# Moving the four tiles of split inputs to byte 352 of their 512-byte period

## The chip, the cores and the metric

One NeuronCore of a Trainium2 chip runs the whole program. The metric is the device time of one execution in microseconds. Lower is better.

## What is computed

One sequence of 256 tokens with 1024 features goes through two transformer blocks in float32. The first has two attentions (stick-breaking and latent), an output projection, a gated feed-forward part with a short convolution, and a gated embedding. The second has a sparse attention, a convolution branch and a memory attention, which are gated and merged, and a gated feed-forward part. Cut to what matters here:

```
h = rms_norm(x) ; proj = h @ w_in ; ... attention ... ; x = x + rms_norm(mix @ w_o)
h = rms_norm(x) ; u = causal_depthwise_conv(h @ w_up)
x = x + rms_norm((gelu(gate) * val) @ w_down)
x = x + rms_norm(sigmoid(rms_norm(x) @ w_ple_gate + b) * (p @ w_ple))
... second block: xn @ w_in, three branches, merged @ w_out ...
x = h + (silu(hn @ w_gate) * (hn @ w_up)) @ w_down
```

Nearly all of the arithmetic is in these products of an activation with a weight matrix.

## The kernel before

Every weight matrix is cut into 128x128 blocks. Eight blocks make one weight tile of 1024 columns, which is loaded into `raw`. ScalarE rounds it to the fp32r type in `whi` (L1109), and VectorE (L1622) or GpSimd (L602) writes what the rounding lost to `wlo`. The activations are split in the same way: ScalarE writes the rounded half (L1132) and VectorE what is left (L1651, L1881, L2245). Both halves of one 128-feature chunk lie side by side in a row of 512 floats, columns 0 to 255 high and 256 to 511 low.

A block product is then three matmuls, of which the weights are the stationary operand and the activation the moving one (256 columns, 1024 bytes per partition):

```
nc.tensor.matmul(dst, wh, hi, ...)   # L619
nc.tensor.matmul(dst, wl, hi, ...)   # L620
nc.tensor.matmul(dst, wh, lo, ...)   # L621
```

The helper `blk3` issues them. TensorE runs its instructions in the order of the program text, and each matmul has a weight load of its own (128 columns, 512 bytes per partition), which the profile lists as PEld. A few stages with the tokens in the rows (`tm`, L662 to L664) have the roles turned round: there the activation is the stationary operand and up to 512 weight columns move.

Four tiles hold split activations:

- `HA`, the normed input of most stages (eight chunks);
- `HB`, a second one of that size (attention outputs, the merged branches);
- `HL`, half as long (latent inputs, the convolution branch, the sparse attention's output);
- `ACTS`, the 22 chunks of feed-forward activations, which shares its place with the attention's tiles (`QS`, `QM`, `Z`, `CW` and others), since those are dead by then.

SBUF tensors are laid one behind the other in the order of the text, each start rounded up to 32 bytes. Tensors that nothing reads (`before_ha`, `before_hb`, `before_hl`, `behind_hl`) stand between them as spacers. Of the addresses this text gives the *phase*: the byte address within the partition, modulo 512. `whi` and `wlo` have phase 128, and since a block is 512 bytes wide, so has every weight block. A chunk of a split tile is 2048 bytes and a half 1024, so all hi and lo operands of one tile have that tile's phase.

| tile | address before | phase before | address after | phase after |
|---|---|---|---|---|
| raw, whi, wlo | 16512, 36992, 61568 | 128 | the same | 128 |
| X, Y, SQ | 87936, 96128, 104320 | 384 | the same | 384 |
| HA | 112960 | 320 | 112992 | 352 |
| HB | 129472 | 448 | 129888 | 352 |
| HL | 146048 | 128 | 146784 | 352 |
| KMEM to identb | 154496 and on | 384 | 155040 and on | 416 |
| ACTS, YC, G1, PX and most attention tiles | 173376 and on | 320 | 173920 and on | 352 |
| QME, U, CY, PR2, OMEM, TH | 200992 and on | 288 | 201536 and on | 320 |

Before, the split tiles and ACTS start at multiples of 64 bytes. Phase 352 is 32 bytes past such a multiple.

Of the kernel before, what the change touches and what calls it, by code (L numbers as in the profile page):

```python
# [16 lines left out]
P = 128  # L17
# [281 lines left out]
def program(nc, stream, xT, memT, pT, pos, consts, w2, out):  # L299
    ctx = ExitStack()  # L300
    with ctx:
        def sb(name, shape, dt=F32):
            return ctx.enter_context(nc.sbuf_tensor(name, shape, dt))
# [9 lines left out]
        X = sb("X", [P, DC, S])  # L313
        Y = sb("Y", [P, DC, S])
        SQ = sb("SQ", [P, DC, S])
        sb("before_ha", [P, 112])
        HA = sb("HA", [P, DC, 2 * S], F32R)
        sb("before_hb", [P, 32])
        HB = sb("HB", [P, DC, 2 * S], F32R)
        sb("before_hl", [P, 48])  # L320
        HL = sb("HL", [P, 4, 2 * S], F32R)
        sb("behind_hl", [P, 64])
        KMEM = sb("KMEM", [P, MEMH, S])
        VMEM = sb("VMEM", [P, QT, 512])
        RTT = sb("RTT", [P, 2, 2 * S])
# [2102 lines left out]
```

## Time and profile before

| what | value |
|---|---|
| median of three executions | 882.14 us (881.25 to 884.82) |
| the profiled execution, its time | 886.73 us |
| its span, first to last instruction | 885.0 us |
| mean granted TensorE clock | 0.988 |
| TensorE matmul busy | 832.1 us, 94% |
| TensorE weight load busy | 794.3 us, 90% |
| VectorE busy | 660.9 us, 75% |
| ScalarE busy | 499.7 us, 56% |
| GpSimd busy | 321.6 us, 36% |

A matmul is on record for longer than it keeps the next one waiting, since matmuls are pipelined. What one costs is read from the distance between two starts, or from the number of them in a stretch in which TensorE never sits idle. A granted clock of 1.00 is the 2.4 GHz level, 0.50 the 1.2 GHz level.

### The profile page before, as it was taken

How to read it: one execution, taken by the hardware profiler on the slowest of the kernel's cores; microseconds unless marked ns; L12 is line 12 of the kernel's file. 1: busy time of each engine (PE TensorE's matmuls, PEld its weight loads, DVE VectorE, ACT ScalarE, POOL GpSimd, SP SyncE). 2: the span in 40 equal slices, each digit the busy share in tenths (PEclk: the TensorE clock that was granted, in tenths of full speed). 3: DMA queues.
4: the chain of work that ended last, by engine and by line, in shares of the span. 5: the costliest groups of instructions: out<-in, count | busy, mean ns of one | idle time of the engine just before them, and what ended most of it. 6: DMA issues, size and time to landing. Idle time of an engine off the chain costs nothing.

```text
span 885.0 us, 16964 instructions
## 1 busy us (share of the span) xinstructions
PE 832.1 (94%) x6722; PEld 794.3 (90%) x6722; DVE 660.9 (75%) x981; ACT 499.7 (56%) x914; POOL 321.6 (36%) x148
## 2 busy tenths in 40 slices
PE   4999999999899999998999889988999999999998
PEld 3998889899899999797999779877998899999998
DVE  6695863898889997657899988865756576667774
ACT  6665645844555666866765574457555545444441
POOL 3743222112332333443656453422454233323321
PEclk8999999999999999999999998999999999999999
DMA  5743234344564756461756452322445457666651
GB/s 206 267 161 98 76 91 141 117 144 158 168 213 149 222 160 190 142 190 49 247 168 201 152 171 73 96 96 72 137 153 168 163 152 224 196 190 192 185 173 49
DMA packets 57246, 137.18 MB, mean 155 GB/s; under 512 B 6352, under 2 KB 27088, under 8 KB 57168
## 3 DMA queue, kind: packets, MB, share of 16 engines
q1 hardware_dynamic: 57168, 136.11, 48.4%
q8 instruction: 53, 0.87, 0.4%
q14 instruction: 25, 0.20, 0.1%
HBM read 135.03 MB, written 1.05 MB: 154 GB/s over the span
## 4 chain that ended last, share of the span: by engine, by line
PE 57%; DVE 23%; ACT 9%; issue 7%; DMA 2%; POOL 1%; SPq 0%; DVEq 0%; ACTq 0%
PE PROD L619 11%; PE PROD L620 10%; PE PROD L621 10%; DVE wlo L1622 6%; DVE YC L1930 5%; ACT whi L1109 4%; DVE RS L1630 3%; PE PROD L681 3%; PE OP L821 2%; DMA raw<-stream 2%; PE OP L619 2%; PE TP L621 2%; PE TP L620 2%; PE TP L619 2%; PE OP L621 2%
## 5 line engine op out<-in xcount | busy, mean ns | idle before, releaser
L602 POOL TENSOR_TENSOR wlo<-raw,whi 128x1024 fp32r<-128x1024 f32 x124 | 318.2, 2572 | 542.8 <-ACT whi L1109 518.6
L619 PE MATMUL PROD<-HA,whi 128*128 128x256 f32 x1080 | 306.8, 284 | 14.4 <-DVE HA L1651 6.0
L620 PE MATMUL PROD<-HA,wlo 128*128 128x256 f32 x1080 | 301.8, 279 | 0.0
L621 PE MATMUL PROD<-HA,whi 128*128 128x256 f32 x1080 | 301.7, 279 | 0.0
L1109 ACT ACTIVATE whi<-raw 128x1024 fp32r<-128x1024 f32 x252 | 261.8, 1053 | 39.7 <-PE PROD L621 21.1
L1622 DVE TENSOR_TENSOR wlo<-raw,whi 128x1024 fp32r<-128x1024 f32 x128 | 192.7, 1510 | 77.8 <-ACT whi L1109 77.7
L619 PEld LDWEIGHTS PROD<-HA,whi 128*128 128x128 f32 x1080 | 205.8, 191 | 17.7 <-DVE HA L1651 6.4
L620 PEld LDWEIGHTS PROD<-HA,wlo 128*128 128x128 f32 x1080 | 205.5, 190 | 0.6 <-issue 0.5
L621 PEld LDWEIGHTS PROD<-HA,whi 128*128 128x128 f32 x1080 | 205.1, 190 | 0.0
L1930 DVE SCALAR_TENSOR_TENSOR YC<-Y,CV,YC 128x255 f32<-128x255 f32 x88 | 66.9, 762 | 2.2 <-ACT YC L1333 0.7
L619 PE MATMUL OP<-HA,whi 128*128 128x256 f32 x200 | 57.2, 286 | 1.5 <-DVE wlo L1622 0.8
L621 PE MATMUL OP<-HA,whi 128*128 128x256 f32 x200 | 56.1, 281 | 0.0
L620 PE MATMUL OP<-HA,wlo 128*128 128x256 f32 x200 | 56.1, 280 | 0.0
L1630 DVE RECIPROCAL RS<-RTT 128x256 f32<-128x256 f32 (+2 forms) x18 | 42.9, 2382 | 15.8 <-ACT RTT L1128 15.7
L619 PE MATMUL SC<-ACTS,whi 128*128 128x256 f32 x176 | 49.1, 279 | 4.1 <-POOL wlo L602 2.4
L681 PE MATMUL PROD<-SQ,ones 128*128 128x256 f32 x144 | 37.3, 400 | 13.2 <-ACT SQ L1121 13.2
L621 PE MATMUL SC<-ACTS,whi 128*128 128x256 f32 x176 | 48.8, 277 | 0.0
L620 PE MATMUL SC<-ACTS,wlo 128*128 128x256 f32 x176 | 48.8, 277 | 0.0
L619 PE MATMUL TP<-ACTS,whi 128*128 128x256 f32 x176 | 48.7, 277 | 0.0
L620 PE MATMUL TP<-ACTS,wlo 128*128 128x256 f32 x176 | 48.7, 277 | 0.0
L621 PE MATMUL TP<-ACTS,whi 128*128 128x256 f32 x176 | 48.7, 277 | 0.0
L681 PEld LDWEIGHTS PROD<-SQ,ones 128*128 128x128 f32 x144 | 26.6, 197 | 21.2 <-issue 10.0
(322 smaller groups left out, 1648.4 us busy)
## 6 DMA issues: line engine op xcount, KB each, us to landing
raw<-stream SPq DMA_DIRECT2D x197, 512.0 KB, 4.0
raw<-stream SPq DMA_DIRECT2D x144, 128.0 KB, 2.4
raw<-stream SPq DMA_DIRECT2D x28, 256.0 KB, 2.9
raw<-stream SPq DMA_DIRECT2D x4, 384.0 KB, 3.4
X<-xT SPq DMA_DIRECT2D x2, 512.0 KB, 5.6
out<-X SPq DMA_DIRECT2D x8, 128.0 KB, 2.0
KMEM<-memT SPq DMA_DIRECT2D x1, 512.0 KB, 5.4
VMEM<-memT SPq DMA_DIRECT2D x1, 512.0 KB, 6.1
```

What stands on the lines that cost most here:

```text
L602: nc.gpsimd.tensor_tensor(wlo[:, n % NSPLIT, :], raw[:, n % NRAW, :], whi[:, n % NSPLIT, :].bitcast(F32), ALU.subtract).then_inc(lo_pool, 1)
L619: nc.tensor.matmul(dst, wh, hi, start=start, stop=False, skip_group_check=True)
L620: nc.tensor.matmul(dst, wl, hi, start=False, stop=False, skip_group_check=True)
L621: last = nc.tensor.matmul(dst, wh, lo, start=False, stop=stop, skip_group_check=True)
L681: last = nc.tensor.matmul(dst[:, 0:w], mat[:, :], chunks[i][:, 0:w], start=i == 0, stop=i == len(chunks) - 1)
L821: last = nc.tensor.matmul(OP[:, j * dv:(j + 1) * dv], PT[0:w, i * P:(i + 1) * P], v, start=kb == 0, stop=kb == nkb - 1, skip_group_check=True)
L1109: nc.scalar.activation(whi[:, n % NSPLIT, :], raw[:, n % NRAW, :], ACT.Copy).then_inc(hi_done, 1)
L1622: nc.vector.tensor_tensor(wlo[:, n % NSPLIT, :], raw[:, n % NRAW, :], whi[:, n % NSPLIT, :].bitcast(F32), ALU.subtract).then_inc(lo_vector, 1)
L1630: nc.vector.reciprocal(dst[:, 0:width], RTT[:, RT[name] % 2, 0:width]).then_inc(rs_ready, 1)
L1930: ins = nc.vector.scalar_tensor_tensor(out=y[:, shift:S], in0=src[:, 0:S - shift], scalar=CV[:, at:at + 1], in1=y[:, shift:S], op0=ALU.mul ...
```

## The change

Only the widths of the four spacers change, so that HA, HB, HL and ACTS all start at phase 352. No instruction is added, removed or moved on any engine, and every tensor behind HA moves up by 32 to 736 bytes.

```diff
         SQ = sb("SQ", [P, DC, S])
-        sb("before_ha", [P, 112])
+        sb("before_ha", [P, 120])
         HA = sb("HA", [P, DC, 2 * S], F32R)
-        sb("before_hb", [P, 32])
+        sb("before_hb", [P, 124])
         HB = sb("HB", [P, DC, 2 * S], F32R)
-        sb("before_hl", [P, 48])
+        sb("before_hl", [P, 124])
         HL = sb("HL", [P, 4, 2 * S], F32R)
-        sb("behind_hl", [P, 64])
+        sb("behind_hl", [P, 16])
         KMEM = sb("KMEM", [P, MEMH, S])
```

## Rows read from the trace of the kernel before

**Rows 1.** The page: busy time by engine, and the chain that ended last.
```profile
span 885.0 us, 16964 instructions
PE 832.1 (94%) x6722; PEld 794.3 (90%) x6722; DVE 660.9 (75%) x981; ACT 499.7 (56%) x914; POOL 321.6 (36%) x148
...
PE 57%; DVE 23%; ACT 9%; issue 7%; DMA 2%; POOL 1%; SPq 0%; DVEq 0%; ACTq 0%
```

**Rows 2.** Groups by line and shape, L619's five: busy, mean ns, idle before.
```profile
L619 PE MATMUL PROD<-HA,whi 128*128 128x256 f32 x1080 | 306.8, 284 | 14.4 <-DVE HA L1651 6.0 <-DVE HA L1881 2.2 <-ACT CW L1477 1.8
...
L619 PE MATMUL OP<-HA,whi 128*128 128x256 f32 x200 | 57.2, 286 | 1.5 <-DVE wlo L1622 0.8 <-DVE KS L1707 0.5 <-DVE HA L1651 0.3
...
L619 PE MATMUL SC<-ACTS,whi 128*128 128x256 f32 x176 | 49.1, 279 | 4.1 <-POOL wlo L602 2.4 <-DVE ACTS L1651 1.5
...
L619 PE MATMUL TP<-ACTS,whi 128*128 128x256 f32 x176 | 48.7, 277 | 0.0
...
L619 PE MATMUL PROD<-HB,whi 128*128 128x256 f32 x160 | 45.4, 284 | 0.0
...
L619 PE MATMUL PROD<-HL,whi 128*128 128x256 f32 x68 | 20.1, 296 | 2.2 <-DVE HB L2245 2.2
```

**Rows 3.** Timeline of TensorE: HB (phase 448), nine steps in 1.02 us.
```profile
679.94 0.28 PE L621 MATMUL PROD<-HB,whi 128*128 128x256 f32 x1
...
680.96 0.28 PE L621 MATMUL PROD<-HB,whi 128*128 128x256 f32 x1
```

**Rows 4.** Timeline of TensorE: HL (phase 128), nine steps in 1.08 us.
```profile
361.84 0.28 PE L621 MATMUL PROD<-HL,whi 128*128 128x256 f32 x1
...
362.92 0.28 PE L621 MATMUL PROD<-HL,whi 128*128 128x256 f32 x1
```

**Rows 5.** Timeline of TensorE: HA (phase 320), nine steps in 1.06 us.
```profile
320.69 0.28 PE L619 MATMUL PROD<-HA,whi 128*128 128x256 f32 x1
...
321.75 0.28 PE L619 MATMUL PROD<-HA,whi 128*128 128x256 f32 x1
```

**Rows 6.** Windows without idle time: busy (count) of PE, PEld, DVE, ACT, POOL, clock.
```profile
44.00:54.80 10.80, 10.80 (x94) 10.80 (x93) 9.40 (x10) 6.92 (x12) 3.45 (x2) 1.00 0.26 90
241.00:257.40 16.40, 16.40 (x142) 16.40 (x141) 14.12 (x21) 9.49 (x14) 4.85 (x2) 1.00 0.61 193
304.00:343.50 39.50, 39.50 (x338) 39.50 (x337) 36.73 (x53) 23.07 (x36) 11.85 (x5) 1.00 0.63 196
372.80:395.00 22.20, 22.20 (x191) 22.20 (x190) 13.13 (x18) 13.88 (x23) 12.16 (x5) 1.00 0.58 174
...
171.80:214.60 42.80, 42.80 (x380) 42.80 (x379) 38.34 (x52) 22.14 (x34) 9.84 (x4) 1.00 0.53 171
704.60:880.00 175.40, 175.40 (x1550) 175.40 (x1550) 122.47 (x157) 75.40 (x104) 48.99 (x20) 1.00 0.57 173
```

**Rows 7.** The window of the merged branches, the same columns.
```profile
545.00:660.00 115.00, 108.90 (x889) 101.28 (x889) 78.21 (x150) 62.41 (x149) 40.86 (x16) 0.98 0.35 111
```

**Rows 8.** Timeline of TensorE where HA gives way to HB.
```profile
640.67 0.28 PE L619 MATMUL PROD<-HA,whi 128*128 128x256 f32 x1
640.79 0.28 PE L620 MATMUL PROD<-HA,wlo 128*128 128x256 f32 x1
640.90 0.28 PE L621 MATMUL PROD<-HA,whi 128*128 128x256 f32 x1
641.01 0.28 PE L619 MATMUL PROD<-HB,whi 128*128 128x256 f32 x1
641.13 0.28 PE L620 MATMUL PROD<-HB,wlo 128*128 128x256 f32 x1
641.25 0.28 PE L621 MATMUL PROD<-HB,whi 128*128 128x256 f32 x1
641.37 0.28 PE L619 MATMUL PROD<-HB,whi 128*128 128x256 f32 x1
```

**Rows 9.** Groups by line and shape: the same work on tiles of different phase.
```profile
L772 PE MATMUL SC<-KMEM,QME 128*128 128x256 f32 x16 | 3.9, 386 | 0.0
...
L681 PE MATMUL PROD<-QM,ones 128*128 128x256 f32 x16 | 3.7, 386 | 1.1 <-ACT QS L1220 1.1
...
L1539 ACT ACTIVATE TH<-PROD 128x256 f32<-128x256 f32 x16 | 6.2, 387 | 17.1 <-PE PROD L621 17.1
...
L2203 DVE SCALAR_TENSOR_TENSOR PROD<-TH,PROD 128x256 f32<-128x256 f32 x8 | 3.4, 430 | 13.3 <-PE PROD L621 12.2 <-ACT TH L1539 1.1
...
L2203 DVE SCALAR_TENSOR_TENSOR PROD<-CW,PROD 128x256 f32<-128x256 f32 x8 | 3.4, 423 | 1.3 <-PE PROD L621 1.3
...
L1477 ACT ACTIVATE CW<-PROD 128x256 f32<-128x256 f32 x8 | 3.1, 383 | 9.8 <-PE PROD L621 9.8
```

## The prediction, made before the changed kernel ran

> **What bounds the kernel now.** I read the page first. TensorE is busy for 832.1 of 885.0 us and holds 57% of the chain that ended last, VectorE 23% and ScalarE 9% [rows 1]. So what counts is the pace of the matmuls. Most are the three of a block product: 1080 + 200 + 176 + 176 + 160 + 68 = 1860 blocks, three matmuls each, so 5,580 of 6,722 [rows 2]. The means of these rows hide the pace, since a matmul is on record for some 280 ns and the next starts long before that. I therefore took the timeline and looked at nine steps from start to start where TensorE never waits. The same instruction has three paces:
>
> - 1.02 us for nine, 113.3 ns each, with HB as the moving operand [rows 3];
> - 1.06 us for nine, 117.8 ns each, with HA [rows 5];
> - 1.08 us for nine, 120.0 ns each, with HL [rows 4].
>
> The windows say how long each lasts. The recorded count takes in two or three matmuls that began before the window, so I take 2.5 off. Then the last 175.4 us and the stretch from 171.8 to 214.6 run at 113.3 ns, and four long stretches (10.8, 16.4, 39.5 and 22.2 us, together 88.9 us) at about 117.8 [rows 6]. All six have HA, and most ACTS too, at phase 320, the clock is granted at 1.00 (the 2.4 GHz level) in all, and DMA, VectorE and ScalarE are as busy in some of the 113.3 ns stretches as in some of the others. So at phase 320 a stream of matmuls has two steady paces, and keeps the one that it falls into after a wait for tens of microseconds. A change of the moving tile's phase alone can switch it: 0.11 us steps with HA become 0.12 us steps at the first HB matmul, with no wait between them [rows 8]. At phase 448 both paces occur too [rows 3, 8], at 128 the step is 120 [rows 4].
>
> **The change, part by part.** No instruction moves. What can change is the pace at which one matmul follows another, and how fast the other engines read and write their shifted tiles.
>
> What is there to win or lose, against 113.3 ns for all:
> - the four stretches at 117.8 ns hold 88.9 / 0.1178 = 755 matmuls, times 4.45 ns = 3.4 us [rows 5, 6];
> - HL has 204 matmuls [rows 2]; times 6.7 ns = 1.4 us [rows 3, 4];
> - from 545 to 660 us HA and HB take turns in short bursts, 889 matmuls in all [rows 7]. If all took 117.8 ns that would be 4.0 us; I estimate half, 2.0 us, and another 0.7 us for short bursts elsewhere.
>
> Together 7.5 us. That is the most that a better phase can give. The most it can take: all 5,580 at 117.8 are 24.8 us over the fast pace, 17.3 us more than now; all at 120.0 are 37.2, 29.7 more than now.
>
> *HA and ACTS, 320 to 352.* The distance from the weights' phase goes from 192 to 224 bytes. No row shows a matmul of this kind whose moving operand starts 32 bytes off a multiple of 64. The bounds are the two above. The nearest row by far is phase 320 itself, 32 bytes away, and it has both paces. The matmuls with QME as the moving operand start at phase 288, also 32 past a multiple of 64, and they cost 386 ns, just as the same shape with QM at 320 [rows 9]; those are plain f32 and pass at half the pace, so they speak against a fixed fee on such a start but can't show a collision of two fast streams. I take no change: 0.0 us.
>
> *HL, 128 to 352.* It leaves the only phase at which a step of 120 ns is the rule. At HA's average, about 114.5 ns (113.3 and 117.8 in the shares above), its 204 matmuls save 1.1 us. Some of them run where TensorE waits for others later anyway; I count 0.8.
>
> *HB, 448 to 352.* 480 matmuls, now at 113.3 ns in long stretches and at 117.8 in the bursts. If it keeps the pace that HA had before it [rows 8], 24 bursts or fewer are spared the switch: 0.5 us, of which 0.3 on the path. Weight loads from HA, HB and HL in the turned stages are about a hundred instructions; a few ns each is 0.3 us either way. I take 0.
>
> *Other engines.* VectorE reads TH (phase 288) in 430 ns and CW (320) in 423 in the same instruction; ScalarE writes TH in 387 and CW in 383 [rows 9]. Seven ns on each of 981 VectorE instructions [rows 1], nearly all of which will have an operand 32 bytes off, is 6.9 us of VectorE, and at its 23% of the chain 1.6 us. Below, it is nothing. The two rows also differ in where their inputs come from, so I take 0 and keep +1.6 for the range. TensorE's own work hides it in the last part, where VectorE is busy 122 of 175 us [rows 6].
>
> Sum: 0 − 0.8 − 0.3 = −1.1 us. Against the profiled execution's 886.73 that is 885.6. That one execution lay 4.6 us above the median of three, which I take as its own scatter, so the forecast for the median is 882.1 − 1.1 = **881.0 us**. A measurement of this kernel tells about 0.5%, 4.4 us, from no change.
>
> On the rule that speaks against any effect: the Trainium skill, "TensorE: Matmul & The Clock Gate", section "Step-by-step: what each phase is for", says that TensorE has two independent read ports on SBUF and that loading the next weights takes nothing from the matmul that runs. By that rule addresses don't matter, and the sum would be 0 and the time 882.1. This trace disagrees: 113.3 and 120.0 ns for one shape at one clock. The rule would still be saved if the pace came from something other than the phase, so it stands among the rivals.
>
> **The rivals.**
> 1. *Phase 352 is like 320* (my forecast): both paces occur, in about today's shares. 881.0, and 878 to 886 with the shares drawn anew. Chance 0.42.
> 2. *The pace has nothing to do with the phase*: 882.1. For it, that 113.3 and 117.8 share a phase. Against it, HL's 120. Chance 0.08.
> 3. *352 is better.* The collision at distance 0 (HL) is the worst, and 224 is further from it than 192, so the 117.8 ns pace may vanish. Of the 7.5 us some 6 lie on the path: 876. Chance 0.22.
> 4. *352 is worse, 117.8 everywhere*: suppose that a fast stream which starts 32 bytes off a multiple of 64, which no row shows, pays a little in each matmul, as HA's does at its 117.8 ns pace. Where TensorE never idles (the last 175 us and the long feed-forward stretch) the loss falls wholly on the span, elsewhere half: 17.3 becomes 14, so 896. It decides as soon as about a third of the matmuls now at 113.3 ns turn to 117.8 (4.4 us / 4.45 ns = 990 matmuls). Chance 0.13.
> 5. *The same with 120.0 everywhere*: 29.7 becomes 25, so 907. Chance 0.06.
> 6. *One long stretch falls into the 117.8 ns pace.* The last 175.4 us are one unbroken stream of some 1,548 matmuls [rows 6], decided by how it starts. If it comes out at 117.8, 1,548 x 4.45 ns = 6.9 us: 888. Chance 0.09, for it is one draw, and most long streams run at 113.3 today.
>
> **How the numbers follow.** The time is rival 1's, 881.0. Faster by over 0.5% (below 877.7) are rival 3 and 0.01 of rival 1: 0.23. Within 0.5% are the rest of rival 1, rival 2 and part of 6: 0.50. Slower: rivals 4 and 5 and most of 6: 0.27. The range reaches over rival 3's low end (875) and up to rival 4 with its VectorE term (898), and leaves out rival 5 and the edges.
>
> **What the profile of the changed kernel would show.** Right: nine steps of an HL matmul take 1.02 or 1.06 us, never 1.08; HA, HB and ACTS show both 1.02 and 1.06; no switch of pace where HB follows HA. The stretch of the last 175 us holds about 1,550 matmuls. Instruction times of VectorE and ScalarE within 2% of now. Wrong: a third pace for HA (then rival 4 or 5, visible as 1,490 or fewer matmuls in those 175 us), or 1.02 everywhere (rival 3), or longer VectorE instructions all over. The prediction fails most easily by that last stream's draw and by the untested 32 bytes.

## The result and the profile after

The changed kernel takes 893.47 us (median of four, 892.56 to 894.04), the kernel before 882.70 in the same measurement (four, 881.25 to 884.82): a ratio of 1.0115, 95% interval 1.009 to 1.014. It is slower. A later measurement with ten executions of the changed kernel and nineteen of the kernel before gives 893.38 against 889.06, ratio 1.006 (1.0025 to 1.0095). The changed kernel is where it was; the kernel before scatters, which becomes part of the story. The ratios, here and below, are the measurement's own estimate and not the quotient of the two medians, and they leave out the executions in the slow state (more than 1.5% above the kernel's fastest).

The page of the kernel after, busy time and chain:

```profile
span 890.8 us, 16964 instructions
PE 844.9 (95%) x6722; PEld 808.4 (91%) x6722; DVE 658.4 (74%) x981; ACT 500.9 (56%) x914; POOL 322.6 (36%) x148
...
PE 64%; DVE 20%; ACT 7%; issue 7%; DMA 1%; DVEq 0%; SPq 0%; ACTq 0%
```

TensorE is busy 12.8 us longer and holds 64% of the chain instead of 57% [rows 1]. Windows of the kernel after; columns as in [rows 6]:

```profile
150.00:345.00 195.00, 191.12 (x1583) 188.47 (x1582) 173.51 (x242) 112.52 (x176) 51.27 (x21) 1.00 0.54 169
...
171.80:214.60 42.80, 42.80 (x364) 42.80 (x363) 37.91 (x51) 22.08 (x33) 10.06 (x4) 1.00 0.51 163
304.00:343.50 39.50, 39.41 (x334) 39.20 (x332) 36.81 (x54) 22.10 (x36) 10.87 (x5) 1.00 0.64 191
...
704.60:880.00 175.40, 175.40 (x1485) 175.40 (x1484) 115.74 (x153) 76.04 (x104) 48.52 (x20) 1.00 0.55 167
```

From 171.8 to 214.6 us there were 380 matmuls and are 364; in the last stretch 1550 and 1485; from 304 us, where [rows 6] had 338, there are 334. So there is now one pace in all of them: 175.4 / (1485 − 2.5) = 118.3 ns. The timeline of the kernel after, ACTS at 740 us and HL at 362 us, nine steps each:

```profile
740.06 0.28 PE L619 MATMUL SC<-ACTS,whi 128*128 128x256 f32 x1
...
741.13 0.28 PE L619 MATMUL SC<-ACTS,whi 128*128 128x256 f32 x1
```

```profile
361.80 0.28 PE L619 MATMUL PROD<-HL,whi 128*128 128x256 f32 x1
...
362.87 0.28 PE L619 MATMUL PROD<-HL,whi 128*128 128x256 f32 x1
```

1.07 us each, 118.9 ns; over a long stream the steps repeat a pattern of eight that averages 118.33. That is slower than HB in [rows 3] and HA in [rows 5], and a little faster than HL in [rows 4].

I also added up, over all block matmuls of a trace, what each distance between two starts below 126 ns (longer ones are waits or the lower clock) has above 113.33 ns. Call it the *excess*: 7.6 us in the first profile before, 27.2 us after. That is 19.6 us more of matmul time, against 10.8 us between the two medians. The two profiled executions are only 5.8 us apart (886.73 and 892.56), because they got the clock differently: by their mean granted clocks (0.988 and 0.996) the one before spent 21.3 us of its span at the 1.2 GHz level and the one after 6.8. A later profile of the kernel before, before_look_1 below, spent 7.1 us there, and is the fairer match: 21.6 us more excess from it to the kernel after, and 12.1 us more span (878.7 to 890.8). Followed matmul by matmul, in program order, 4.3 us of these 12.1 have come about when the last stream starts, and 7.8 us come in it: TensorE never idles there, and 1,562 matmuls at 5.0 ns more fall wholly on the span. The first feed-forward part shows the other case. From 150 to 345 us the kernel before has this window:

```profile
150.00:345.00 195.00, 187.51 (x1587) 183.67 (x1585) 173.21 (x241) 111.86 (x176) 52.28 (x21) 1.00 0.54 170
```

TensorE idled 7.5 of 195 us and idles 3.9 now, for nearly the same number of matmuls (1587 and 1583): VectorE, busy 173 us in both, sets most of the time there, and the slower matmuls mainly filled waits. In the chain that ended last, cut to this window, VectorE's L1930 has 25% both before and after, and no line of TensorE over 2%. Of the 5.6 us that the excess grows by in the window, about 1 us shows up as time: from the 900th matmul of the program to the 2,400th the kernel after takes 1.0 us longer.

The same-work groups of [rows 9] in the kernel after:

```profile
L1539 ACT ACTIVATE TH<-PROD 128x256 f32<-128x256 f32 x16 | 6.2, 388 | 16.6 <-PE PROD L621 16.6
...
L772 PE MATMUL SC<-KMEM,QME 128*128 128x256 f32 x16 | 3.9, 386 | 0.0
...
L2203 DVE SCALAR_TENSOR_TENSOR PROD<-TH,PROD 128x256 f32<-128x256 f32 x8 | 3.4, 430 | 14.0 <-PE PROD L621 12.9 <-ACT TH L1539 1.1
...
L2203 DVE SCALAR_TENSOR_TENSOR PROD<-CW,PROD 128x256 f32<-128x256 f32 x8 | 3.4, 422 | 1.3 <-PE PROD L621 1.3
```

TH has left and CW has taken a start 32 bytes off a multiple of 64, and both are read in the time that they took. Writing CW (L1477) takes 387 ns after 383, four nanoseconds on eight instructions. The other engines show no cost. (L772 says nothing of the distance: its two operands, KMEM and QME, moved together.)

### The profile page after: what moved, and what is told of

Same layout as the page of the kernel before. It is cut to its first block, busy times and chain, and to the rows that moved or that the text cites. A ratio compares the mean times of both kernels' runs of the same rounds, so it can differ in the third digit from the quotient of the medians.

```text
span 890.8 us, 16964 instructions
## 1 busy us (share of the span) xinstructions
PE 844.9 (95%) x6722; PEld 808.4 (91%) x6722; DVE 658.4 (74%) x981; ACT 500.9 (56%) x914; POOL 322.6 (36%) x148
## 4 chain that ended last, share of the span: by engine, by line
PE 64%; DVE 20%; ACT 7%; issue 7%; DMA 1%; DVEq 0%; SPq 0%; ACTq 0%
PE PROD L619 13%; PE PROD L621 12%; PE PROD L620 12%; DVE YC L1930 6%; DVE wlo L1622 5%; PE PROD L681 3%; ACT whi L1109 3%; PE OP L821 2%; DVE RS L1630 2%; PE OP L619 2%; PE OP L620 2%; PE OP L621 2%; PE TP L619 1%; PE TP L621 1%; PE TP L620 1%
## 5 line engine op out<-in xcount | busy, mean ns | idle before, releaser
L619 PE MATMUL PROD<-HA,whi 128*128 128x256 f32 x1080 | 308.8, 286 | 13.9 <-DVE HA L1651 6.2
L620 PE MATMUL PROD<-HA,wlo 128*128 128x256 f32 x1080 | 304.0, 281 | 0.0
L621 PE MATMUL PROD<-HA,whi 128*128 128x256 f32 x1080 | 303.9, 281 | 0.0
L1622 DVE TENSOR_TENSOR wlo<-raw,whi 128x1024 fp32r<-128x1024 f32 x128 | 187.7, 1469 | 76.2 <-ACT whi L1109 76.2
L619 PEld LDWEIGHTS PROD<-HA,whi 128*128 128x128 f32 x1080 | 204.1, 189 | 17.3 <-DVE HA L1651 6.8
L620 PEld LDWEIGHTS PROD<-HA,wlo 128*128 128x128 f32 x1080 | 204.3, 189 | 0.6 <-issue 0.5
L621 PEld LDWEIGHTS PROD<-HA,whi 128*128 128x128 f32 x1080 | 204.1, 189 | 0.0
L1930 DVE SCALAR_TENSOR_TENSOR YC<-Y,CV,YC 128x255 f32<-128x255 f32 x88 | 66.9, 762 | 2.2 <-ACT YC L1333 0.7
L619 PE MATMUL OP<-HA,whi 128*128 128x256 f32 x200 | 57.2, 286 | 0.6 <-DVE KS L1707 0.5
L620 PE MATMUL OP<-HA,wlo 128*128 128x256 f32 x200 | 56.2, 281 | 0.0
L621 PE MATMUL OP<-HA,whi 128*128 128x256 f32 x200 | 56.2, 281 | 0.0
L619 PE MATMUL SC<-ACTS,whi 128*128 128x256 f32 x176 | 49.6, 282 | 2.2 <-POOL wlo L602 1.2
L681 PE MATMUL PROD<-SQ,ones 128*128 128x256 f32 x144 | 37.3, 401 | 12.9 <-ACT SQ L1121 12.8
L619 PE MATMUL TP<-ACTS,whi 128*128 128x256 f32 x176 | 49.4, 281 | 0.0
L620 PE MATMUL TP<-ACTS,wlo 128*128 128x256 f32 x176 | 49.4, 281 | 0.0
L621 PE MATMUL TP<-ACTS,whi 128*128 128x256 f32 x176 | 49.4, 281 | 0.0
L620 PE MATMUL SC<-ACTS,wlo 128*128 128x256 f32 x176 | 49.4, 281 | 0.0
L621 PE MATMUL SC<-ACTS,whi 128*128 128x256 f32 x176 | 49.4, 281 | 0.0
L619 PE MATMUL PROD<-HB,whi 128*128 128x256 f32 x160 | 46.1, 288 | 0.0
```

The source lines that it names most:

```text
L619: nc.tensor.matmul(dst, wh, hi, start=start, stop=False, skip_group_check=True)
L620: nc.tensor.matmul(dst, wl, hi, start=False, stop=False, skip_group_check=True)
L621: last = nc.tensor.matmul(dst, wh, lo, start=False, stop=stop, skip_group_check=True)
L681: last = nc.tensor.matmul(dst[:, 0:w], mat[:, :], chunks[i][:, 0:w], start=i == 0, stop=i == len(chunks) - 1)
L1622: nc.vector.tensor_tensor(wlo[:, n % NSPLIT, :], raw[:, n % NRAW, :], whi[:, n % NSPLIT, :].bitcast(F32), ALU.subtract).then_inc(lo_vector, 1)
L1930: ins = nc.vector.scalar_tensor_tensor(out=y[:, shift:S], in0=src[:, 0:S - shift], scalar=CV[:, at:at + 1], in1=y[:, shift:S], op0=ALU.mul ...
```

## The experiments

Below, *distance* is the phase of the moving tile minus that of the weights (128 unless said), modulo 512.

**Is it the start 32 bytes off a multiple of 64, or the distance?** All tiles, the weights too, move up by 32:

```diff
+        sb("before_raw", [P, 8])
         raw = sb("raw", [P, NRAW, TILE])
```

> The spacers of before, and one more of 32 bytes ahead of raw, so that the weights (phase 160) and every tile behind them move up by 32: HA and ACTS are at 352 as in the change, HB at 480, HL at 160, and all distances to the weights are those of before. Theory D, only the distance between the moving operand and the weights counts: HA and ACTS keep two paces, 113.3 and 117.8 ns, HL 120, time 882 within 3 us. Theory M, the start 32 bytes off a multiple of 64 costs by itself: about 118.3 ns everywhere as in the changed kernel, time 893.

885.4 us against 885.8, ratio 0.9977 (0.994 to 1.001). HA and ACTS at phase 352 run at 113.3 and 117.8 ns, HL at 120, excess 8.0 us. ACTS in that kernel, nine steps in 1.02 us:

```profile
739.98 0.28 PE L620 MATMUL SC<-ACTS,whi 128*128 128x256 f32 x1
...
741.00 0.28 PE L620 MATMUL SC<-ACTS,whi 128*128 128x256 f32 x1
```

The phase 352 is harmless with the weights at 160: HA and ACTS start there in this kernel and in the changed one, and only with the weights at 128 do they take 118.3. Theory M falls, the distance counts.

**Which tiles?** Two halves of the change:

```diff
-        sb("before_ha", [P, 112])
+        sb("before_ha", [P, 120])
         HA = sb("HA", [P, DC, 2 * S], F32R)
-        sb("before_hb", [P, 32])
         HB = sb("HB", [P, DC, 2 * S], F32R)
-        sb("before_hl", [P, 48])
         HL = sb("HL", [P, 4, 2 * S], F32R)
-        sb("behind_hl", [P, 64])
+        sb("behind_hl", [P, 8])
```

That is h_tiles_352, with ACTS left at 320. In acts_352 only ACTS moves:

```diff
-        sb("behind_hl", [P, 64])
+        sb("behind_hl", [P, 72])
```

> HA, HB and HL at phase 352, everything behind them (ACTS too) back at the phases of before. If the pace hangs on the moving tile alone: matmuls with HA, HB and HL at 118.3 ns; those with ACTS at 113.3 or 117.8, or at whatever pace HA hands on to them. If it were a matter of the tiles of the other engines behind HL (YC, G1, RS, RTT), time and paces would be those of before, 882. First theory: of the 10.8 us the most stays, since HA has 3,840 of the matmuls: 888 to 893.

> HA, HB and HL at the phases of before, ACTS and all tiles behind HL as in the changed kernel. By the moving-tile theory only the 1,056 matmuls with ACTS go to 118.3 ns, HA keeps its two paces: about 5 us of matmul time more at most, 884 to 887. By the theory that the other engines' tiles matter: near 893 with HA's matmuls slowed too.

h_tiles_352: 891.8 us, ratio 1.0061 (1.002 to 1.010). HA, HB and HL take 118.2 to 118.3 ns on average, ACTS 114.3. acts_352: 889.3, above the expected 884 to 887, but its ratio 1.0021 (0.9986 to 1.0056) can't be told from no change; ACTS takes 118.2, HA 114.7, HL 119.5. Each tile carries its own pace, even inside one stream where HA and ACTS alternate. The windows from 710 to 875 us, first h_tiles_352, then acts_352:

```profile
710.00:875.00 165.00, 165.00 (x1413) 165.00 (x1412) 111.28 (x147) 73.75 (x101) 46.15 (x19) 1.00 0.58 176
```

```profile
710.00:875.00 165.00, 165.00 (x1432) 165.00 (x1431) 113.67 (x147) 70.46 (x97) 46.29 (x19) 1.00 0.56 174
```

**A map of the distance.** Since each tile has its own pace, one kernel tries four phases. The edits of map_even, map_odd_a and map_odd_b (changed lines only, as in the diffs below):

```diff
-        sb("before_ha", [P, 112])
-        sb("before_hb", [P, 32])
+        sb("before_hb", [P, 80])
-        sb("before_hl", [P, 48])
+        sb("before_hl", [P, 16])
-        sb("behind_hl", [P, 64])
+        sb("behind_hl", [P, 80])
```

```diff
-        sb("before_ha", [P, 112])
+        sb("before_ha", [P, 8])
-        sb("before_hb", [P, 32])
+        sb("before_hb", [P, 16])
-        sb("before_hl", [P, 48])
+        sb("before_hl", [P, 16])
-        sb("behind_hl", [P, 64])
+        sb("behind_hl", [P, 80])
```

```diff
-        sb("before_ha", [P, 112])
+        sb("before_ha", [P, 48])
-        sb("before_hb", [P, 32])
+        sb("before_hb", [P, 8])
-        sb("before_hl", [P, 48])
+        sb("before_hl", [P, 16])
-        sb("behind_hl", [P, 64])
+        sb("behind_hl", [P, 32])
```

> Four phases at once, all multiples of 64: HA 384 (256 bytes from the weights), HB 192 (64), HL 256 (128), ACTS 0 (384). By theory M (only the 32 bytes off 64 hurt, and distance 0): 113.3 or 117.8 at all four, time 876 to 886. By theory D with a smooth course over the distance: 256 is furthest from 0 and is the best or, after 224 came out worse than 192, the worst; HB at 64 is nearer HL's 120.

> Distances to the weights of 288 (HA), 352 (HB), 416 (HL) and 160 bytes (ACTS), all 32 off a multiple of 64. So far: 0 and 256 give 120 ns, 64 gives 117.8, 128 and 384 give 118.7, 192 and 320 give 113.3 or 117.8, 224 gives 118.3. Theory P, the pace has a period of 256 bytes in the distance and the odd multiples of 32 lie between their neighbours: HA 117 to 119, HB and ACTS 116 to 118.5, HL as ACTS. Theory R, the pace is random from phase to phase: no order, and one of the four may be 113.3 throughout. Time 888 to 896 by P.

> Distances of 448 (HA), 480 (HB), 32 (HL) and 96 bytes (ACTS). Theory P, period 256: HA as at 192, so 113.3 and 117.8 both, HB as at 224, 118.3, HL as at 288, ACTS as at 352. If HA keeps two paces the time is near 882 to 888. Theory R: HA's pace at 448 isn't that at 192.

The paces, as means over twelve or nine consecutive starts inside streams without a wait; where a tile shows several, the most frequent one or the range:

| distance modulo 256 | seen at | step, ns |
|---|---|---|
| 0 | 0 (HL before), 256 (HA, map_even) | 119.3 to 120.0; 120.0, some 118.5 to 119.8 |
| 32 | 32 (HL, map_odd_b), 288 (HA, map_odd_a) | 116.7; 116.7, some 118 |
| 64 | 64 (HB, map_even), 320 (HB before) | 117.8; 113.3 or 117.8 |
| 96 | 96 (ACTS, map_odd_b), 352 (HB, map_odd_a) | 120.0 and 120.0, some 118.8 to 119.9 |
| 128 | 128 (HL, map_even), 384 (ACTS, map_even) | 118.2 to 119.2, both |
| 160 | 160 (ACTS, map_odd_a), 416 (HL, map_odd_a) | 117.1 to 120.1; 117.0 to 119.1 |
| 192 | 192 (HA, ACTS before), 448 (HA, map_odd_b) | 113.3 or 117.8, both |
| 224 | 224 (all, the change), 480 (HB, map_odd_b) | 118.3 and 118.3 |

In every row the two distances 256 apart show the same paces or overlapping ones, which fits theory P's period; theory R falls. The row of 160 is the loosest, and one tile at each distance is little. Theory P's other half, that the odd multiples of 32 lie between their neighbours, fails: 64 and 192 are the only residues at which 113.3 was seen, and a step of 32 bytes from either loses it. The times: map_even 899.4 us, ratio 1.0145 (1.007 to 1.022), excess 32.9 us; map_odd_a 892.7, ratio 1.0056 (1.0025 to 1.0087); map_odd_b 888.7, 0.9998 (0.997 to 1.003), 0.7 us over what was expected. Two rows of the map in the timeline, nine steps in 1.08 us both: HA at 256 in map_even,

```profile
434.03 0.28 PE L618 MATMUL PROD<-HA,whi 128*128 128x256 f32 x1
...
435.11 0.28 PE L618 MATMUL PROD<-HA,whi 128*128 128x256 f32 x1
```

and ACTS at 96 in map_odd_b.

```profile
725.01 0.28 PE L619 MATMUL SC<-ACTS,whi 128*128 128x256 f32 x1
...
726.09 0.28 PE L619 MATMUL SC<-ACTS,whi 128*128 128x256 f32 x1
```

**Which weight load does a matmul collide with?** Only wlo moves, to phase 64:

```diff
+        sb("before_wlo", [P, 112])
         wlo = sb("wlo", [P, NSPLIT, TILE], F32R)
...
-        sb("before_ha", [P, 112])
```

> Only wlo moves, from phase 128 to 64 (X, Y and SQ go from 384 to 320 with it); the split tiles stay where they were before. Theory L, a matmul collides with the weight load that runs beside it, which is the next one: wlo is loaded beside the matmuls of L619, one in three, and is now 256 bytes from HA and ACTS. These cost 120, the two others 113.3 or 117.8: mean 115.5 or more, and the gaps differ by line. Theory O, each matmul collides with its own weights (wlo: those of L620): then the gap behind L620 is the long one. Theory A, only the moving tile's own address counts: the paces of before, 113.3 and 117.8 alike on all three lines.

896.1 us, ratio 1.0073 (1.004 to 1.0105), excess 23.4. HA and ACTS take 117.8 nearly everywhere, and on all three lines (HA: 117.9, 117.6 and 118.1 ns behind L619, L620, L621). With HB, 320 bytes from whi and 384 from wlo, the three differ: 116.5, 113.9, 118.3. HL, 0 bytes from whi and now 64 from wlo, went from 119.6 to 117.7. The split tiles did not move, so theory A falls: the weights' address takes part. But neither L nor O foresees equal gaps for HA and such unequal ones for HB. Whether a load and a matmul collide at all, and which with which, stays open; these gaps look like a property of the whole cycle of three and not like a sum of fees.

X, Y and SQ moved too, and no run moves them alone. In every other kernel here their phase is the weights' plus 256, so with a period of 256 the map can't tell the distance to the weights from the distance to them. The traces speak against them. The block matmuls read none of the three, and the pace doesn't hang on whether an engine that could is at work: in the kernel after, ACTS takes 118.4 ns in the 190 steps in which VectorE is idle and 118.3 in the 777 in which it is busy, and 118.3 in the 97 in which VectorE, ScalarE and GpSimd are all idle; in map_even HA takes 119.9 and 119.8 (VectorE idle in 749 steps, busy in 2,574).

**One phase for all four tiles.** all_320 and all_320_again are one kernel, with this edit:

```diff
-        sb("before_hb", [P, 32])
-        sb("before_hl", [P, 48])
-        sb("behind_hl", [P, 64])
+        sb("behind_hl", [P, 16])
```

all_448 and all_64 have the same three lines and one more, with 16 in all_448 and 48 in all_64:

```diff
-        sb("before_ha", [P, 112])
+        sb("before_ha", [P, 16])
```

after_again is the changed kernel itself, timed beside all_64.

> All four split tiles at phase 320, 192 bytes from the weights, other tiles as before. HL leaves 120 for 113.3 or 117.8, 1.2 us less matmul time, and no change of phase where HB follows HA, so that HB keeps HA's pace, up to 0.9 us less. Time 880 to 882 against 882 to 886; within what can be told of no change. By a theory that any phase behaves alike: no difference in HL's pace, 120.

> All four at 448, 320 bytes from the weights, which is 64 modulo 256. Both paces are known from HB. By the period of 256 that the maps show, it has 113.3 and 117.8 as 320 has; HB at 192 (64 bytes) showed 117.8 alone. If 113.3 is as likely as at 320, the time is that of all_320, 882 to 886; if 117.8 is the rule, 17 us more matmul time than 113.3 throughout would be seen as 890 to 893.

> All four at phase 64, 448 bytes from the weights, which is 192 modulo 256 as at 320. By the period of 256: 113.3 and 117.8 as in the version with all at 320, never a third pace, some 1,458 matmuls from 710 to 875 us if the last stream draws 113.3, 1,403 if 117.8; time 880 to 888. Against the period: another pace, or a time of 890 and more.

> The changed kernel once more, beside executions of the kernel before on the same chip. Its one pace of 118.3 ns leaves nothing to draw: 891 to 895 again. The kernel before is expected at 883 to 892 there, so that the ratio is nearer 1.005 than the first measurement's 1.0115.

| kernel | distance | median, us | ratio to before | matmuls from 710 to 875 us |
|---|---|---|---|---|
| all_320 | 192 | 882.7 | 0.9909 (0.988 to 0.994) | 1459 |
| all_320_again | 192 | 881.7 | 0.9928 (0.990 to 0.996) | 1458 |
| all_64 | 448 | 883.4 | 0.9953 (0.991 to 0.9994) | 1458 |
| all_448 | 320 | 896.8 | 1.0137 (1.007 to 1.020) | 1403 |
| after_again | 224 | 893.4 | 1.0060 (1.0025 to 1.0095) | 1397 |

all_64 has 113.3 and 117.8 as its only lasting paces, as the period demands. all_448 came out above the expected 882 to 893: of 254 pieces of twelve steps with HA, three run at 113.3 and the others at 117.3 or more, though HB had run at 113.3 for long stretches at that phase [rows 3], and HL, in this same kernel, does so in four of its nine pieces. So a distance of 64 modulo 256 allows 113.3 but HA hardly enters it there. At 192, eight of the nine profiles of kernels with HA and ACTS both there (before and its four repeats, all_320 twice, all_64, all_up_32) have the last stream at 113.3.

**Why does the kernel before scatter?** The four executions of all_448 lie within 0.5 us and the four of map_even within 3.2, those of the changed kernel within 1.5 in the first measurement (four) and 4.0 in the second (ten), those of wlo_64, which has almost one pace, within 6.0 (ten). The kernel before runs from 880 to 893. Four more executions of it, unchanged, each with its profile:

> The kernel before, unchanged, once more. Its executions have spread from 880 to 896 us, while the changed kernel's lay within 1.5 us. Theory W, the spread is the choice between the two paces at phase 320: other streams will be at 117.8 ns than in the first profile, and the time is about 878 us plus the part of the 117.8 ns streams that lies on the path; if the last stream of 1,560 takes 117.8, the time is near 889. Theory C, the spread is the clock: the paces are those of the first profile and the granted clock differs.

> The same once more, to see the draw change from one execution to the next. Theory W: the list of streams at 117.8 ns is another one than in the two profiles so far. Theory C: the same list.

> The kernel before, once more. The two looks gave 880.4 and 884.4 us, with little at 117.8 ns and none of it in the last stream of 1,560 matmuls in the first. Wanted is an execution of 889 or more. Theory W: the last stream, or as many matmuls in others, is then at 117.8 ns. Theory C: the paces are as in the other looks.

> The same again. If the time is below 885, the last stream is at 113.3 by theory W; if above 888, at 117.8.

880.4, 884.4, 879.2 and 887.4 us, with an excess of 5.6, 9.7, 10.8 and 17.1 us. The windows of the first and the fourth:

```profile
710.00:875.00 165.00, 165.00 (x1458) 165.00 (x1457) 113.19 (x148) 70.39 (x97) 45.02 (x19) 1.00 0.57 174
```

```profile
710.00:875.00 165.00, 165.00 (x1403) 165.00 (x1402) 108.26 (x146) 71.08 (x97) 44.63 (x19) 1.00 0.57 171
```

In before_look_4 the last stream drew 117.8. These two are a clean pair: 7.1 and 3.6 us at the lower clock, and the last stream starts at 698.2 us in both. Its first matmul and its last, first in before_look_1, then in before_look_4:

```profile
698.24 0.28 PE L620 MATMUL OP<-HA,wlo 128*128 128x256 f32 x1
...
875.16 0.28 PE L621 MATMUL TP<-ACTS,whi 128*128 128x256 f32 x1
```

```profile
698.22 0.28 PE L620 MATMUL OP<-HA,wlo 128*128 128x256 f32 x1
...
882.08 0.28 PE L621 MATMUL TP<-ACTS,whi 128*128 128x256 f32 x1
```

The same 1,562 matmuls take 6.9 us more, 1,562 x 4.45 ns, and that is the whole difference of the spans (878.7 and 885.6). So what one draw costs is shown; that it is behind the spread of all the other executions, of which no trace was kept, is inferred from their times. Of the nineteen beside after_again five lie from 879.8 to 884.3 and fourteen from 888.4 to 893.3, none between, and the clock doesn't make that gap: at one mean granted clock, 0.994, there are 879.8, 880.4, 882.0 and 888.4. But the gap is in this set alone; each of the four other sets has times between, the 25 beside map_even for example 885.1, 885.5, 885.8, 886.4 and 887.4. Shorter streams draw too (before_look_3 has 10.8 us of excess, none of it in the last stream). And if every time above 888 were a slow draw, about half of the executions would have one, where only one profile of five shows it.

The clock has as large a share in single executions. The first profile before has its last stream at 113.3, in 176.9 us just as before_look_1, and still ends 6.3 us behind it: that stream starts at 704.5 instead of 698.2, after 21.3 us at the lower clock against 7.1. So theory C has its part in the spread, but it doesn't choose between 1458 and 1403.

> All four split tiles at 320 once more, on another chip. It came out 0.9% faster than the kernel before, while its certain gains, HL off 120 ns and HB's turns, are 1 to 2 us. Either the six executions were lucky draws: then this time 0.1 to 0.3% faster and a spread like that of before, 880 to 892. Or the streams fall to 113.3 more surely when no tile of another phase comes before them: then again 0.7% or more.

all_320 is faster than the kernel before a second time. Its fourteen executions lie from 880.0 to 885.8, none at 888 or more, so its last stream seems to draw 113.3 far more surely; two profiles show it and the other times imply it. HL at 115.7 and 117.1 ns instead of 119.6 and one phase for HB save 0.7 to 1.6 us of excess; why the draw gets better is open. all_64 has the same distance modulo 256, and of its ten executions nine lie from 879.7 to 885.3 and one at 892.4.

**Can the draw be forced?** ACTS at 448, the three others at 320:

```diff
-        sb("before_hb", [P, 32])
-        sb("before_hl", [P, 48])
-        sb("behind_hl", [P, 64])
+        sb("behind_hl", [P, 48])
```

> HA, HB and HL at 320, ACTS and what is behind it at 448 (320 bytes from the weights). Theory K, a step from phase 320 to 448 sends the stream to 117.8 and the step back to 113.3, as at 641 us of the kernel before: then in both feed-forward stages HA runs at 113.3 and ACTS at 117.8 in turn, whatever a wait began with; ACTS has 1,056 matmuls, 4.7 us more, and the spread between executions gets small; time 881 to 885. Theory W without K: a stream keeps its pace over the change of tile.

885.0 us (882.7 to 888.8), ratio 0.999 (0.9955 to 1.0026). The timeline of acts_448 at the two changes of tile:

```profile
720.13 0.28 PE L618 MATMUL PROD<-HA,wlo 128*128 128x256 f32 x1
720.24 0.28 PE L619 MATMUL PROD<-HA,whi 128*128 128x256 f32 x1
720.35 0.28 PE L617 MATMUL SC<-ACTS,whi 128*128 128x256 f32 x1
720.47 0.28 PE L618 MATMUL SC<-ACTS,wlo 128*128 128x256 f32 x1
720.59 0.28 PE L619 MATMUL SC<-ACTS,whi 128*128 128x256 f32 x1
...
726.01 0.28 PE L617 MATMUL OP<-HA,whi 128*128 128x256 f32 x1
726.12 0.28 PE L618 MATMUL OP<-HA,wlo 128*128 128x256 f32 x1
726.24 0.28 PE L619 MATMUL OP<-HA,whi 128*128 128x256 f32 x1
726.35 0.28 PE L617 MATMUL OP<-HA,whi 128*128 128x256 f32 x1
```

In the whole last stream ACTS takes 117.8 and HA 113.3, turn by turn, 1439 matmuls from 710 to 875 us. Theory K holds there: the change of phase sets the pace. In the first feed-forward part it holds at each change inside a stream, but a stream that begins with HA after a wait may start at 117.8, so HA averages 114.6 there. It buys certainty at 4.6 us of excess for ACTS, and the spread, 6.1 us, is not as small as expected.

## Why the prediction was wrong

**The step that failed** is "*HA and ACTS, 320 to 352* ... I take no change: 0.0 us", and its reason, "The nearest row by far is phase 320 itself, 32 bytes away". Nearness in bytes says nothing here. The two paces of distance 192 are gone at 224, and one pace of 118.3 ns took their place. HA's excess went from 4.5 to 18.7 us and that of ACTS from 0.9 to 5.3: 18.6 us of matmul time in a term that was sized 0. With 1.3 for HB and 0.3 back from HL that is the 19.6 measured. The account of the kernel before was right, 7.5 us over the fast pace where 7.6 were measured. The time lies inside the stated range (875 to 898), but on the side to which the prediction gave 0.27. What in the hardware makes the distance count stays open.

**The rival that came true** is the fourth, "*352 is worse, 117.8 everywhere*", with 118.3 for 117.8. Its mechanism was wrong: not the start 32 bytes off a multiple of 64 (all_up_32 has it and pays nothing) but the distance to the weights. Its price on the path was too high, 14 us of 17.3; measured were 10.8 between the medians and 12.1 of 21.6 against before_look_1. (A side sum there is off: the 990 matmuls that would decide are a quarter of the some 4,000 then at 113.3 ns, not a third.) The last stretch fell wholly on the span as said (7.8 us). For "the long feed-forward stretch" this was wrong: VectorE bounds most of it. Before, TensorE idled 7.5 us there, which the prediction didn't ask about.

**HL.** "Its 204 matmuls save 1.1 us": the direction is right, HL left 120 for 118.3, and the excess fell from 1.2 to 0.9 us. The pace named (1.02 or 1.06 us for nine) didn't come.

**HB.** No switch where HB follows HA: true, but both are at 118.3, so 0.5 us of gain became 1.3 us of loss (excess 1.0 to 2.3).

**Other engines, taken at 0.** Right: the groups above stand where they stood, VectorE is busy 658.4 us after 660.9.

**The rule on two independent read ports.** The Trainium skill, "TensorE: Matmul & The Clock Gate", section "Step-by-step: what each phase is for", has the next weight load take nothing from the running matmul. By rival 2, which the prediction rested on it, nothing should have changed. The traces disagree with that: at one shape and one clock the step goes from 113.3 or 117.8 to 118.3 ns when HA moves to 352 with HB and HL and the weights stay (h_tiles_352), to 120.0 at 384 (map_even), and back to 113.3 or 117.8 with HA at 352 when the weights move to 160 (all_up_32). That the weight load is what takes the time from the matmul is not shown.

**The median of before as a base.** The prediction took 4.6 us between the profiled execution and the median as scatter without asking what scatters. In that execution it was the clock, 21.3 us at the lower level, and not a draw. Rival 6 had seen the draw, as a thing of the changed kernel: in the last stream it is 6.9 us. It is a property of the kernel before, and the changed kernel has lost it. Against the nineteen later executions of the kernel before the change costs 0.6%, against the first four, none of which is above 885, 1.2%.

## What to carry to other kernels

Where TensorE streams fp32r matmuls of 256 columns back to back, look at the distance between consecutive starts before anything else, tile by tile: the mean duration in a group hides it. If two tiles or two stretches with the same instruction differ, it is worth mapping the pace over the difference of the two operands' addresses, modulo 256 bytes; one kernel with a different phase for each tile maps several at once. Before comparing two profiles, take how long each spent at the lower clock, and compare those that match. Don't interpolate between phases, and don't trust a few executions of a kernel whose streams have two paces: here one draw is 0.8% of the time. And ask of each stretch what bounds it: here the slower matmuls cost their full price in the last stream, where TensorE never waits, and about a fifth of it in the first feed-forward part, which VectorE bounds.

## What was not expected of the hardware

- The pace of a matmul stream depends on the distance between the operands' addresses with a period of 256 bytes as far as the sixteen distances show: 120.0 ns at 0 and 96, 118.2 to 119.2 at 128, 117 to 120 at 160, 118.3 at 224, mostly 116.7 at 32, and 113.3 only at 64 and 192 (the same instruction, granted clock 1.00).
- At 64 and 192 a stream has two lasting paces, 113.3 and 117.8 ns. It keeps one for 1,562 matmuls (before_look_1 and before_look_4); after a wait either can come, a change between tiles of one phase leaves it (all_320), a change of the tile's phase can switch it, and between 320 and 448 the pick is nearly fixed (HA 113.3, ACTS 117.8 in acts_448).
- At the lower clock (granted 0.50, 1.2 GHz), as from 21.7 to 23.2 us in the kernel before, six steps of HA take 1.28 us: 213.3 ns each, 256 columns at 1.2 GHz with nothing on top. The distance doesn't count there: HA's steps at the lower clock average 213.3 ns at 224 (39 steps, h_tiles_352), at 256 (63 steps, map_even) and at 288 (29 steps, map_odd_a). The timelines, first the kernel before, then map_even with HA at 256, whose step is 120.0 at the higher level:

```profile
21.78 0.41 PE L619 MATMUL PROD<-HA,whi 128*128 128x256 f32 x1
...
23.06 0.41 PE L619 MATMUL PROD<-HA,whi 128*128 128x256 f32 x1
```

```profile
20.22 0.41 PE L620 MATMUL PROD<-HA,whi 128*128 128x256 f32 x1
...
21.50 0.41 PE L620 MATMUL PROD<-HA,whi 128*128 128x256 f32 x1
```
